# Two feed-forward networks in a four-layer block: token-major products with 512 moving columns instead of feature-major products with 256

## The reference

```python
FFN_HIDDEN = -(-8 * D_MODEL // (3 * 256)) * 256      # 2816
def swiglu_layer(x, norm_g, w_gate_up, w_down):
    h = rmsnorm(x, norm_g)
    g, u = jnp.split(h @ w_gate_up, 2, axis=-1)
    return x + (jax.nn.silu(g) * u) @ w_down
```

## Time and profile before

| | |
|---|---|
| time, median of 3 runs | 2014.77 us (2014.64 to 2015.54) |
| profiled execution: its span, first to last instruction | 2016.7 us |
| TensorE busy | 1938.2 us, 96% |
| VectorE busy | 1325.4 us, 66% |
| ScalarE busy | 714.0 us, 35% |
| mean granted TensorE clock | 0.989 of 2.4 GHz |

### The profile page before, as it was taken

How to read it: one execution, slowest core, us unless ns; L and a number is a source line. 1 busy time by engine, 2 the same in 40 slices (tenths; PEclk the granted TensorE clock), 3 DMA queues, 4 the chain that set the end, 5 groups by cost and what they waited for, 6 DMA issues and landing times.

```text
span 2016.7 us, 41700 instructions
## 1 busy us (share of the span) xinstructions
PE 1938.2 (96%) x18103; PEld 1790.5 (89%) x18103; DVE 1325.4 (66%) x1722; ACT 714.0 (35%) x1023; POOL 76.7 (4%) x123
## 2 busy tenths in 40 slices
PE   7999999999899999999998999998999999999998
PEld 7988999998599999989887879997998887889997
DVE  8896687646648766864675339575764776428764
ACT  5573433434533332240423123243222234214243
POOL 2000000000400000010000000000002000000000
PEclk9999999999999999999999999998999999999999
DMA  8545477943347885645440236453663550135543
GB/s 219 142 140 157 152 255 255 272 130 116 95 149 241 265 245 126 162 122 148 124 116 4 65 106 169 124 164 95 172 168 94 148 135 25 45 105 147 157 126 105
DMA packets 473064, 291.43 MB, mean 145 GB/s; under 512 B 26679, under 2 KB 467484, under 8 KB 472776
## 3 DMA queue, kind: packets, MB, share of 16 engines
q1 hardware_dynamic: 466688, 262.20, 46.7%
q0 software_dynamic: 5312, 25.32, 3.3%
q10 hardware_dynamic: 904, 1.58, 0.3%
HBM read 288.02 MB, written 1.05 MB: 143 GB/s over the span
## 4 chain that ended last, share of the span: by engine, by line
PE 80%; DVE 13%; ACT 3%; issue 2%; DMA 1%; POOL 0%; DVEq 0%; ACTq 0%; SPq 0%
PE bank L705 38%; PE bank L1408 5%; PE bank L1410 5%; PE bank L1409 5%; PE bank L694 4%; PE bank L664 2%; DVE rounded L730 2%; PE bank L887 2%; PE bank L879 2%; PE bank L787 1%; PE bank L1611 1%; PE bank L1598 1%; PE bank L1054 1%; DMA whole<-in_ffn_w_down 1%; PE bank L1579 1%
## 5 line engine op out<-in xcount | busy, mean ns | idle before, releaser
L705 PE MATMUL bank<-rounded 128*128 128x256 f32 (+1 forms) x4584 | 564.5, 284 | 9.7 <-DVE rounded L730 7.1
L705 PEld LDWEIGHTS bank<-rounded 128*128 128x128 f32 (+1 forms) x4584 | 550.0, 189 | 19.2 <-DVE rounded L730 12.3
L730 DVE TENSOR_TENSOR rounded<-arena,rounded 128x1024 fp32r<-128x1024 f32 (+1 forms) x251 | 303.2, 1213 | 91.7 <-ACT rounded L719 85.6
L1408 PE MATMUL bank<-parts 128*128 128x256 f32 x1024 | 290.5, 284 | 2.2 <-DVE parts L2212 2.2
L1409 PE MATMUL bank<-parts 128*128 128x256 f32 x1024 | 289.8, 283 | 0.0
L1410 PE MATMUL bank<-parts 128*128 128x256 f32 x1024 | 289.8, 283 | 0.0
L705 PE MATMUL bank<-common,arena 128*128 128x256 f32 x1280 | 285.4, 380 | 0.0
L705 PEld LDWEIGHTS bank<-common,arena 128*128 128x128 f32 x1280 | 240.1, 189 | 39.8 <-issue 4.8
L770 ACT ACTIVATE arena<-bank 128x512 f32<-128x512 f32 x114 | 67.7, 597 | 436.4 <-PE bank L705 423.8
L1408 PEld LDWEIGHTS bank<-parts 128*128 128x128 f32 x1024 | 196.5, 192 | 3.0 <-DVE parts L2212 1.6
L1409 PEld LDWEIGHTS bank<-parts 128*128 128x128 f32 x1024 | 196.6, 192 | 0.1
(11 more groups left out here) (391 smaller groups left out, 2498.2 us busy)
## 6 DMA issues: line engine op xcount, KB each, us to landing
arena<-in_w_in SPq DMA_DIRECT2D x190, 512.0 KB, 3.8
whole<-in_ffn_w_gate_up SPq DMA_DIRECT2D x44, 1024.0 KB, 5.2
arena<-in_ada_w POOLq DMA_DIRECT2D x32, 768.0 KB, 6.7
whole<-in_ffn_w_down SPq DMA_DIRECT2D x16, 1408.0 KB, 7.2
arena<-in_rec_w_in SPq DMA_DIRECT2D x36, 512.0 KB, 3.8
arena<-in_att_w_qkv SPq DMA_DIRECT2D x24, 512.0 KB, 3.8
arena<-in_rec_w_out SPq DMA_DIRECT2D x16, 512.0 KB, 3.8
arena<-in_mla_w_o SPq DMA_DIRECT2D x16, 512.0 KB, 4.1
```

Source lines behind the costliest of these rows:

```text
L705: last = pe.matmul(psum[s][0:c, m % 2 * T:m % 2 * T + T], w[a][:, k, cols], x[b][:, k, :], start=(k, a, b) == (0, 0, 0), stop=k == job.kt ...
L730: dve.tensor_tensor(raw_view(job_of[u], u, UNIT_LOW), raw, high_view(job_of[u], u).bitcast(F32), ALU.subtract)\
L1408: pe.matmul(bank, w_hi, x_hi, start=start and k == 0, stop=False)
```

## The change

The two networks now keep the tokens on the partitions of their results. The stationary operand is a 128x128 tile of the input (128 features by 128 tokens), and the weights move, 512 columns a matmul.

- Up: bank `psum[t]` belongs to token half `t` and holds 256 gate columns and 256 up columns side by side. Slot `s` now holds four of the eight feature tiles, gate and up columns together (two DMAs of 512 KB). 12 matmuls for each slot and token half.
- The token scale is one number per partition (`RSTD`, 128x2), so it enters silu as ACT's scale (L2323 of the changed kernel) and the gating as DVE's scalar (L2251), one instruction per token half.
- `hidden` is token-major and must be feature-major for the down product: four transposes per turn (`turn_hidden_pe`, L1415), from whose bank ACT writes the high and DVE the low part.
- Down: `w_down` comes in 11 fills of two row tiles by 1024 columns (1 MB in rows of 4 KB). 24 matmuls per fill go to four banks: two token halves by two column halves. All of X's features finish in the last fill. ACT then copies the four banks to `DOWN_TOK`, 32 transposes in all for both networks (`turn_down_pe`, L1436) bring them back to feature-major, and DVE adds them to X in four pairs.
- The sums of squares for the networks' norm take X's squares as stationary and a single column of ones as moving (`token_pair_pe`).
- The loops are written out.

```diff
-        def three_passes(bank, weights, m, n, x, start, stop):
-            for k in range(n):
-                w_hi, w_lo = (w[:, k, m] for w in weights)
-                x_hi, x_lo = (e[:, k, :] for e in x)
-                pe.matmul(bank, w_hi, x_hi, start=start and k == 0, stop=False)
-                pe.matmul(bank, w_hi, x_lo, start=False, stop=False)
-                last = pe.matmul(bank, w_lo, x_hi, start=False, stop=stop and k == n - 1)
+        def up_products_pe(s, t, ks=range(DK // 2)):
+            for k in ks:
+                for a, b in PASSES:
+                    last = pe.matmul(psum[t], H_PARTS[a][:, 4 * s + k, t * P:t * P + P], UP_W[s][b][:, k, :],
+                                     start=(s, k, a, b) == (0, 0, 0, 0), stop=(s, k, a) == (1, 3, 1))
...
+        def turn_hidden_pe(l, j):
+            for t in range(TT):
+                pe.wait_ge(up_evicted[t].sem, l * UPS + j + 1)
...
+            for m in range(2):
+                for t in range(TT):
+                    last = pe.transpose(bank[:, m * T + t * P:m * T + t * P + P], hidden[:, t, m * P:m * P + P], ident)
...
+            for s in range(2):
+                up_products_pe(s, 1).then_inc(slot_used[s].sem, 1)
+            for j in range(1, UPS):
+                pe.wait_ge(lo_ready[0].sem, up_fill(l, 0, j) + 1)
+                pe.wait_ge(up_evicted[0].sem, l * UPS + j)
+                up_products_pe(0, 0)
+                turn_hidden_pe(l, j - 1)
+                pe.wait_ge(up_evicted[1].sem, l * UPS + j)
+                up_products_pe(0, 1).then_inc(slot_used[0].sem, 1)
+                pe.wait_ge(lo_ready[1].sem, up_fill(l, 1, j) + 1)
+                up_products_pe(1, 0).then_inc(first_tokens_full.sem, 1)
+                up_products_pe(1, 1).then_inc(slot_used[1].sem, 1)
...
+            for t in range(TT):
+                down_products_pe(u, bank, t, (0,), True).then_inc(down_half_full.sem, 1)
+            down_products_pe(u, bank, 0, (1,), True).then_inc(upper[0][2], 1)
+            pe.wait_ge(down_kept.sem, 4 * l + 2)
+            turn_down_pe(0)
+            last = down_products_pe(u, bank, 1, (1,), True)
+            last.then_inc(upper[1][2], 1)
+            pe.wait_ge(down_kept.sem, 4 * l + 4)
+            turn_down_pe(1)
...
         def att_pe():
-            pe.wait_ge(evicted[0].sem, (ffn_down[0].at + DK) // 2)
             first_units_by_pieces(att_q, first_split, 2)
...
+            token_rms_act(D)
             for j in range(UPS):
-                up_turn(j, j < UPS - 1)
+                next_fill(0, j)
+                act.wait_ge(first_tokens_full.sem, l * UPS + j + 1)
+                gate_tokens(0)
+                act.wait_ge(slot_used[1].sem, up_fill(l, 1, j) + 1)
+                gate_tokens(1)
+                next_fill(1, j)
+                hidden_high(j)
             logarithms_act()
```

More of the change, by code:

```diff
@@ L788, in sums_pe, with token_pair_pe @@
                 last.then_inc(done, 1)
+        def token_pair_pe(bank, sq, k):
+            pe.wait_ge(act_squares.sem, act_squares.due(pe))
+            for kk in (k, k + 1):
+                for t in range(TT):
+                    last = pe.matmul(bank[:, t:t + 1], sq[:, kk, t * P:t * P + P], ones[:, 0:1], start=(kk, t) == (0, 0), stop=kk == DK - 1, skip_group_check=True)
+            return last
         def sum_pair_pe(bank, sq, k, nt):
@@ L1027, in program @@
         second = [second_jobs(l) for l in range(2)]
[L1028 to L1032, removed]
         at, job_of = 0, []
@@ new lines, in down_products_pe, with turn_down_pe @@
+        def down_products_pe(u, bank, t, cs, ends=False):
+            for kk in range(2):
+                k = 2 * u + kk
+                for a, b in PASSES:
+                    for c in cs:
+                        last = pe.matmul(bank[t][c], HIDDEN_PARTS[a][:, k, t * P:t * P + P], DOWN_W[u % 2][b][:, kk, c * 512:c * 512 + 512],
+                                         start=(k, a, b) == (0, 0, 0), stop=ends and kk == 1 and a == 1)
+            return last
+        def turn_down_pe(c):
+            for i in range(2):
+                bank, free, done = vbanks.fill()
+                pe.wait_ge(free.sem, free.due(pe))
+                for n in range(2):
+                    for t in range(TT):
+                        at = c * 512 + (2 * i + n) * P
+                        last = pe.transpose(bank[:, n * T + t * P:n * T + t * P + P], DOWN_TOK[:, t, at:at + P], ident)
+                last.then_inc(done, 1)
@@ L1440, in ffn_pe @@
[L1440 to L1450 removed]
+                last = up_products_pe(k // 4, 0, (k % 4, k % 4 + 1))
@@ new lines, in ffn_pe @@
+            upper = [abanks.fill() for _ in range(TT)]
+            for _, free, _ in upper:
+                pe.wait_ge(free.sem, free.due(pe))
+            bank = [[psum[t], upper[t][0]] for t in range(TT)]
+            for u in range(UPS - 1):
+                pe.wait_ge(lo_ready[u % 2].sem, down_fill(l, u) + 1)
+                pe.wait_ge(hidden_ready.sem, l * UPS + u + 1)
+                for t in range(TT):
+                    if u == 0:
+                        pe.wait_ge(up_evicted[t].sem, (l + 1) * UPS)
+                    last = down_products_pe(u, bank, t, range(2))
+                    if (u, t) == (0, 1):
+                        turn_hidden_pe(l, UPS - 1)
+                last.then_inc(slot_used[u % 2].sem, 1)
@@ L2342, in ffn_act @@
             if l == 0:
                 high_act(att_q.first + 1)
-            next_input(DK // 2 - 1)
+            for t in range(TT):
+                act.wait_ge(down_half_full.sem, 2 * l + t + 1)
+                keep_down(t, 0, psum[t])
+            upper = [abanks.empty() for _ in range(TT)]
+            for t in range(TT):
+                bank, full, free = upper[t]
+                act.wait_ge(full.sem, full.due(act))
+                keep_down(t, 1, bank)
+                act.wait_ge(down_kept.sem, 4 * l + 3 + t)
+                act.nop().then_inc(free.sem, 1)
+                free.due(act)
+                if t == 0:
+                    next_high(0)
@@ L2346, in square_heads_v @@
+            square_pair_act(0)
+            for i in range(1, 4):
+                next_high(i)
+                square_pair_act(i)
         def square_heads_v(x, sq):
```

331 lines of the change are left out of this document (136 added, 195 removed).

## The result

| | before | changed |
|---|---|---|
| time, median (lowest to highest) | 2015.15 us (2014.64 to 2015.99, 4 runs) | 2024.76 us (2023.03 to 2026.27, 4 runs) |
| ratio, with its 95% interval | | 1.0041 (1.0029 to 1.0054) |
| span of the profiled execution | 2016.7 us | 2021.2 us |
| the two networks in it | 385.4 us | 388.0 us |

The change makes the kernel slower, by 0.3 to 0.5%. The forecast was 2000 us, with a range that ended at 2016, and both are wrong.

The account below looks back on a forecast made before the run. TensorE's pace was taken to bound the networks. Savings of 33.6 (products) and 4.6 (old waits) against 13.1, 4.8, 2.2, 2.4 and 1.0 us of costs gave -14.7 us: 2000 us, 80% range 1993 to 2016.

Parts of the forecast that it names:

- Products: In both networks, 1584 products of 512 columns at 218 ns replace 3168 of 256: 33.6 us saved.
- rival A: In the networks' products, the 13 ns beside the columns stay (226 ns): saving 20.9 us, time 2013 us; chance 18%.
- old waits: TensorE's waits in the networks of the kernel before, mainly the down stage, go away: 4.6 us saved.
- 120 transposes: The added transposes in both networks, at 109 ns each, all on TensorE: 13.1 us more.
- first turn: Up stage's turn 1 waits for slot 0's bank after only 12 covering products: 2.4 us, twice, 4.8 more.
- into and through the down stage: Fill 2 waits 1.1 us per network behind ACT's table load, 2.2 more; slow DMA loads add 1.0.
- end, inside the borders: At each network's end, TensorE idles before the last transposes for ACT's copy of the last bank: 0.85 us, twice.
- end, third piece of the next layer: After the first network, L664's third piece is ready at 7.5 where TensorE comes at 6.8: 0.7 us more.
- B: Rival: the up turn's chain is late, half a microsecond over in each of 20 turns: 6 us more, 2006; 14%.
- C: Rival: TensorE's clock falls at the first turn's idle time and the end, four times 1.6 us: 2006; 8%.
- D: Rival: weight loads decide, landing in 9 us in most turns, each slot 1.6 us late: 32 us, 2032; 7%.
- E: Rival: the networks' products cost in proportion to columns (239 ns), so no saving: 2034; 5%.

Follow-up runs that it names:

- pace: A separate kernel of nothing but streams of products of one kind each, computing nothing of the reference; fp32r went at 226.7 ns for 512 columns, 119.8 for 256.
- turn_twice: The changed kernel with each transpose of the hidden tiles made twice into the same place; ratio to the kernel before 1.0074 (1.0058 to 1.0089).
- the changed kernel again: The changed kernel, unaltered, profiled and timed again on another chip; ratio to the kernel before 1.0032 (1.0022 to 1.0042).
- down_only: Up stage as in the kernel before, down stage as in the changed kernel; ratio to the kernel before 0.9982 (0.9973 to 0.999), 2015.20 us.
- halves: The changed kernel with each 512-column product as two of 256 with the same stationary tile; ratio to the kernel before 1.0109 (1.0091 to 1.0126).

## Why the prediction was wrong, step by step

**What bounds the kernel: right.** TensorE's pace, count and waits decided; DVE lost 35 us of busy time and nothing came of it.

**Products: the step that failed.** "So where streaming is longer than the load, the load disappears", and from it "I take 218, near the fp32 row". The type was treated as if it didn't matter: the plain fp32 stream has 2.5 ns beside its columns at 215.8 ns, and fp32r has 13 at 256 and at 512 columns. What the 16-column row suggested, that fewer stationary columns make the product cheaper, is true at 256 columns (113.3 ns) and false at 512 (231.1). The saving is 1584 x (240.0 - 226.7) = 21.1 us, 12.5 below the forecast. This is rival A, whose bound of 226 is what `pace` and the timeline show, and that it was given 18% while 218 was given half was the mistake in the chances.

**A alone does not give the result.** Its 2013 us lay inside the range, and faster than before. From its -2.0 to the +2.6 us of the borders, and 0.9 more in the next layer, it takes the smaller misses of the table. The one that was a misreading: the count of 836 gave 119.6 ns for 120.0, so that 1584 pairs were 1.3 us too cheap and the remainder called old waits was 4.6 instead of 385.4 - 380.2 - 1.7 = 3.5 us (3.2 of waits, and late first products behind the sums).

**The other terms**, for the two networks together in the first profile of each kernel. They are read from start to start. A wait costs more than the idle time in its row: 0.16 us for the end of the last record, which the prediction names, and 0.1 for the first product behind a pause (335 ns to the next start instead of 227).

| term | forecast | measured |
|---|---|---|
| products | -33.6 | -21.1 |
| old waits | -4.6 | -3.2, four of 0.7 to 0.9 in the down stages |
| 120 transposes | +13.1 | 22 x 0.48 + 32 x 0.11 = +14.1 |
| first turn | +4.8 | 2 x 2.5 = +5.0, and 1.5 of slow clock |
| into and through the down stage | +2.2 and +1.0 | +2.1 and +1.7 |
| end, inside the borders | +1.7 | +1.8 |
| end, third piece of the next layer | +0.7 | +0.9, outside the borders |
| late load in the up stage | | +0.3 |
| sum inside the borders | -15.4 | +2.2; the borders give +2.6 |

The page gives 2.4 us of idle time before L1424 and 4.6 before L1402, the source of the waits. The wait before fill 2 comes from the place foretold (ACT's table load at 360.00, then the high part), at 1.05 us where 1.1 was forecast; the first turn's wait comes from its place too, at 2.4 where 2.4 was forecast, before the 0.1 of its first product. The third piece of the next layer waits 0.58 us (the row at 422.84), and its 48 products last 6.8 us from the first start to the last end, where they lasted 5.92 before.

**Late loads** show where they were expected, in ACT's waits (waited for, us in total, times, longest), most of them for the down weights:

```profile
ACT parts L2303 <- DMA whole<-in_ffn_w_down: 15.0, 3, 5.8
ACT parts L2303 <- DMA whole<-in_ffn_w_gate_up: 2.8, 1, 2.8
```

These are the waits of the first network. Of ACT's 17.8 us TensorE sees 2.0: three late starts of 0.4 to 0.9 us in the down stage, and one of 0.3 in the up stage (at 273.2), too short for a row.

**Rivals.** A was the case. B did not occur: from the third turn on, turns of 11.35 to 11.37 us follow each other in both networks, but around the late load, with gating at 480 ns where 482 was taken. C occurred in a small way: the clock fell behind the first turn's wait in the first network in both profiles of the changed kernel, for 1.5 us each time, and in the second network in neither. `turn_twice` shows the same, its 12 products behind 2.25 us taking 4.58. D and E did not occur. "Slower" was given 14%, for D, E and mishaps that add up; it came out of A with such mishaps on top.

**Outside the networks.** The ratios stand for 8.3 us (5.8 to 10.9, the result) and 6.5 us (4.4 to 8.5, the changed kernel again). The spans of the profiles differ by 4.5 and 5.8 us: 2.6 and 4.8 in the networks, 0.9 both times behind the first network in the wait told above, and 1.0 and 0.1 elsewhere. So the profiles are nearly explained, but both profiled executions of the changed kernel were faster than the median of theirs (2023.03 against 2024.76, 2022.82 against 2024.16). In the profiles all other stages together take 1633.2 and 1631.3 us in the changed kernel, 1631.3 and 1630.3 before. They differ most where TensorE's clock has fallen, and that differs between executions of one program: the same 48 one-column products of the changed kernel behind the second network are, in its first profile,

```profile
774.55 8.14 PE L1499 MATMUL bank<-common,arena 128*128 128x1 f32 x48
```

and in the one taken again

```profile
775.31 6.55 PE L1499 MATMUL bank<-common,arena 128*128 128x1 f32 x48
```

Whether the change makes such stretches likelier in the executions that have no profile, or the intervals cover the rest (8.3 against 4.5 us, 6.5 against 5.8), no run here tells. It stays open.

**Where the up stage's gain goes** is the rest of the answer, by the first profile. Token-major up products save 1056 x 13.3 = 14.0 us. The hidden tile's transposes take 10.6 back, the first turn's waits 5.0, its clock 1.5 and the late load 0.3: a loss of 3.4. The down stage saves 7.0 by pace and 3.2 of old waits, and pays 3.5 for transposes, 1.8 at the end, 3.8 of new waits and 0.9 in the next layer, which leaves 0.2. `down_only` keeps the second without the first, and its down stage waits only 0.3 us on the way: that is why it gains.

## What to carry to other kernels

Before a forecast rests on the pace of a form that the trace does not have, read whether the nearest row has the same type, and put the bound, not the hope, in the middle where it hasn't: here 9 ns a product, 13.8 us, were nearly the whole gain of 14.7. Read a pace inside a stream and from starts: over whole groups it came out 2.5 ns too high, and by a count of records that touch a window 0.4 ns too low. A wider product saves only the fixed cost of the ones it replaces, and a change of layout that needs transposes on the bound engine pays for each in full, and for the way back to products; count both per turn (11.52 us before, 11.36 after) before anything else. Where a rebuild has parts, take those whose gain is free of the other's price: the down stage needed its transposes once per network, the up stage in every turn.

## What the runs showed that was not expected

- fp32r products have 13 ns beside their columns at 256 and 512 columns (119.8 and 226.7 ns) and 13 to 16 between, bf16 and plain fp32 products 2.5. In the kernel with its transfers it is the same 226.7.
- Behind transposes or plain fp32 the first fp32r product of 512 columns takes 0.31 us to the next start instead of 0.23, so a group of four transposes costs 0.48 us and not 0.42.
- Fewer stationary columns made an fp32r product faster at 256 columns (113.3 against 119.8 ns) and slower at 512 (231.1 against 226.7).
- Behind a wait of 2.25 us, with TensorE busy before, 12 products took 4.46, 4.58 and 4.58 us in the first network (`turn_twice` is the third) and 2.98 and 2.99 in the second, where the wait was as long; behind 1.23 us they took 3.01. In `halves` the wait was 2.09 us, and the same work behind it, 24 products of 256 columns, took 3.11.
